# Five of nine modulation vectors as dot products on the vector engine, with their weights transposed and the attention heads' steps in another order

## The reference

```python
mod = silu(c) @ w_ada + b_ada                    # 6 vectors of 1024: sh1 sc1 g1 sh2 sc2 g2
h = rmsnorm(x, norm1_g) * (1 + sc1) + sh1
q, k, v, u = split(h @ w_in)                     # 4 heads with two maps each; u goes to the SSM
att = softmax(q0 k0) - lam * softmax(q1 k1)      # causal
attn_out = rmsnorm(att @ v, subln_g) * (1 - lambda_init)
z = gelu(ssm(u));  ssm_out = z * sigmoid(z @ w_glu + b_glu)
x = x + g1 * (concat(attn_out, ssm_out) @ w_out)
h = rmsnorm(x, norm2_g) * (1 + sc2) + sh2
x = x + g2 * moe(h)                              # 32 experts, each token goes to its top 4
x = rmsnorm(x, final_g)
shift, scale, gate = split(silu(c_2) @ w_mod_2 + b_mod_2)     # 3 more vectors
...                                              # second block: RG-LRU, dilated attention, merge
return rmsnorm(x + gate * (merged @ w_o), g_final_2)
```

## Time and profile before

| | us |
|---|---|
| median of 3 runs | 2116.95 (2116.36 to 2120.26) |
| profiled execution | 2112.3, span 2111.0 |
| PE busy | 2021.6 (96%) |
| DVE busy | 583.1 (28%) |
| ACT busy | 410.5 (19%) |

### The profile page before, as it was taken

The page is one execution under the profiler, slowest core; times in us unless marked ns, Lnnn a source line. Parts: engine busy times, 40 slices in busy tenths (PEclk is TensorE's granted clock), DMA queues, the critical chain, the costliest instruction groups (busy, mean ns, idle before and its releaser), DMA issues.

```text
span 2111.0 us, 36756 instructions
## 1 busy us (share of the span) xinstructions
PE 2021.6 (96%) x16085; PEld 908.0 (43%) x16085; DVE 583.1 (28%) x1166; ACT 410.5 (19%) x849; POOL 53.0 (3%) x54
## 2 busy tenths in 40 slices
PE   7999998999999999999999999989999999999998
PEld 3454444333443333434334334355444444444443
DVE  4994434211111111101101111142454444300002
ACT  2212432110111010101101101012333353300001
POOL 0000000000000000000000000030000000000000
PEclk9999999999999999999999999989999999999999
DMA  8455795999899999999999999971222211122201
GB/s 321 140 193 192 268 340 222 401 420 363 326 415 413 411 404 415 409 410 402 408 413 406 408 410 416 407 269 72 92 72 66 73 62 64 55 76 80 76 34 70
DMA packets 107153, 553.80 MB, mean 262 GB/s; under 512 B 12848, under 2 KB 24112, under 8 KB 57200
## 3 DMA queue, kind: packets, MB, share of 16 engines
q1 hardware_dynamic: 86880, 517.36, 61.9%
q10 hardware_dynamic: 14560, 17.28, 2.4%
q0 software_dynamic: 5552, 16.78, 2.3%
HBM read 526.73 MB, written 26.35 MB: 262 GB/s over the span
## 4 chain that ended last, share of the span: by engine, by line
PE 67%; SPq 16%; DMA 13%; DVE 2%; ACT 2%; issue 1%; POOL 0%; ACTq 0%; DVEq 0%; POOLq 0%
SPq L374 15%; PE psum L834 15%; PE psum L1007 13%; PE psum L1014 10%; PE psum L503 7%; PE psum L842 6%; DMA arena<-in_w 6%; DMA ring<-in_w 3%; PE psum L1077 3%; PE psum L967 2%; PE psum L476 1%; DMA ring<-in_mod_slabs 1%; DMA ring<-in_v_slabs 1%; PE psum L828 1%; PE psum L1055 1%
## 5 line engine op out<-in xcount | busy, mean ns | idle before, releaser
L834 PE MATMUL psum<-arena,ring 128*32 128x512 f32 x4096 | 452.9, 593 | 19.5 <-DMA arena<-in_w 19.0
L1007 PE MATMUL psum<-h_t,ring 128*128 128x512 f32 x640 | 278.6, 592 | 0.2 <-ACT arena L1383 0.2
L834 PEld LDWEIGHTS psum<-arena,ring 128*32 128x32 f32 x4096 | 134.4, 110 | 333.7 <-issue 331.3
L842 PE MATMUL psum<-arena,h_t 128*32 128x256 f32 x3840 | 217.4, 383 | 8.6 <-DMA arena<-in_w 7.4
L1310 ACT ACTIVATE ring<-psum,mods,gain 128x64 f32<-128x64 f32 (+2 forms) x264 | 85.8, 430 | 647.4 <-PE psum L820 647.4
L1879 DVE TENSOR_SCALAR h_t<-psum 128x512 f32<-128x512 f32 (+2 forms) x33 | 27.9, 845 | 613.8 <-PE psum L834 613.8
L1007 PEld LDWEIGHTS psum<-h_t,ring 128*128 128x128 f32 x640 | 120.4, 190 | 146.4 <-issue 145.9
L842 PEld LDWEIGHTS psum<-arena,h_t 128*32 128x32 f32 x3840 | 123.2, 111 | 93.8 <-DMA arena<-in_w 12.8
L834 PE MATMUL psum<-ring 128*32 128x512 f32 x1344 | 149.2, 593 | 6.4 <-DMA ring<-in_w 6.4
L503 PE MATMUL psum<-h_t,ring 128*128 128x512 f32 x256 | 116.1, 608 | 5.6 <-ACT h_t L1128 5.6
L1014 PE MATMUL psum<-h_t,ring 128*128 128x512 f32 x256 | 112.6, 593 | 1.4 <-ACT work L1192 1.4
(11 more groups left out here) (426 smaller groups left out, 1681.4 us busy)
## 6 DMA issues: line engine op xcount, KB each, us to landing
arena<-in_w SPq DMA_DIRECT2D x288, 1024.0 KB, 28.4
ring<-in_w SPq DMA_DIRECT2D x96, 1024.0 KB, 29.9
ring<-in_mod_slabs SPq DMA_DIRECT2D x16, 2048.0 KB, 9.1
ring<-in_turn_slabs SPq DMA_DIRECT2D x40, 512.0 KB, 3.4
ring<-in_merge_slabs SPq DMA_DIRECT2D x32, 512.0 KB, 3.3
ring<-in_proj_slabs SPq DMA_DIRECT2D x24, 512.0 KB, 3.7
y_rows<-arena SPq DMA_DIRECT2D x1, 10752.0 KB, 35.4
y_rows<-work ACTq DMA_DIRECT2D x70, 64.0 KB, 7.8
```

Of the source, the lines that this page charges most:

```text
L834: mm = pe.matmul(psum[32 * j:32 * j + 32, g, :], x_e[:, c * tokens + g * TG:c * tokens + g * TG + TG], slot[s][:, j * S:(j + 1) * S], star ...
L842: mm = pe.matmul(psum[32 * j:32 * j + 32, 6 + g // 2, (g % 2) * 256:(g % 2) * 256 + 256], h_e[:, g * 256 + half * P + 32 * c:g * 256 + hal ...
L1007: mm = pe.matmul(psum[:, bank, :], ring[:, s, k, :], h_t[:, k, :], start=(k == 0), stop=(k == KT - 1))
```

## The change

Modulations 0 to 3 stay as they were (`ROWS_TO = 4`). For 4 to 8 the weights come transposed (`dot_slabs`, 40 of 128x1024: one output feature on each partition, the 1024 inputs along it). PE spreads each of the two conditions over all partitions (`c_row`), ACT keeps it in `ring` slots 10 and 11, and DVE makes each column of `mods` with one multiply and add over 1024 elements (`dots`), 18 among the heads and 22 in the mix loop. The 40 loads go through slots 4 to 7 one at a time.

```diff
-TURN = 3
-TURNS = 7
+TURN = 7
+TURNS = 3
+        c_rows = [ring[:, 10 + n, :, :].rearrange("p k n -> p (k n)") for n in range(2)]
-        early = [arena[:, 4096 * n:4096 * n + 4096] ...
+        early = [arena[:, 8192 * n:8192 * n + 4096] ...
-        MIX_AT = [4, 5, 2, 3, 0, 1, 2, 3]
+        MIX_AT = [4, 6, 2, 3, 0, 1, 2, 3]
# SP
-            for i in range(12):
-                load_slab_of(8 + i)
-                load_mod_half((i + 5) // 2, (i + 5) % 2)
-            load_mod_half(8, 1)
-            (zeroing of y_rows in one transfer)
+            for n, at in zip(range(8, 11), ((2, 1), (3, 0), (3, 1))):
+                load_slab_of(n)
+                load_mod_half(*at)
+            def load_dots(*numbers):
+                for n in numbers:
+                    if n < 4:
+                        sp.wait_ge(sem("mod halves used"), len(MOD_HALVES))
+                    else:
+                        sp.wait_ge(sem("dots"), n - 3)
+                    sp.dma_start(ring[:, 4 + n % 4, :, :], io["dot_slabs"][n]...).then_inc(sem(f"slot {4 + n % 4} loaded"), 16)
+            load_slab_of(11)
+            load_dots(0, 1, 2, 3)
+            for n in range(12, 16):
+                load_slab_of(n)
             sp.wait_ge(sem("arena zeroed"), 1)
+            clear_blocks(0, 6)
+            load_slab_of(16)
+            load_dots(4, 5, 6, 7)
+            load_slab_of(17)
+            clear_blocks(6, 12)
+            load_dots(8, 9, 10, 11)
+            load_slab_of(18)
+            clear_blocks(12, MAXO)
+            load_dots(12, 13, 14, 15)
+            load_slab_of(19)
...
-            sp.wait_ge(sem("mod turned"), 18)
-            load_first(0, 1, 2, 3, 4, 5)
+            sp.wait_ge(sem("s5 y"), 4)
+            load_first(0, 2)
+            load_dots(16, 17, 18, 19)
+            load_first(3, 8)
+            load_dots(20, 21, 22, 23)
+            load_first(9)
+            load_dots(24, 25, 26, 27)
+            sp.wait_ge(sem("glu"), 4)
+            load_first(1)
             sp.wait_ge(sem("head mixed"), 4)
-            for n in range(20, 23):
+            for n in range(20, 24):
                 load_slab_of(n)
-            load_slab_of(23)
-            load_first(7, 8, 9, 6, 10, 11)
+                if n < 23:
+                    load_dots(*range(4 * n - 52, 4 * n - 48))
+            load_first(6, 10, 11)
+            sp.wait_ge(sem("dots"), 8 * (9 - ROWS_TO))
+            load_first(4, 5, 7)
# PE: first norm
-            pe.wait_ge(sem("tables loaded"), 16)
-            for _ in range(6): (product of 256 columns, not read)
-            rms_sum(0, h_t)
+            pe.wait_ge(sem("ready for idle products"), 1)
+            for _ in range(8): (product of 256 columns of zeros, not read)
+            pe.wait_ge(sem("tables loaded"), 16)
+            for k in range(KT):
+                pe.wait_ge(sem("norm squares"), k + 1)
+                mm = square_sum(k, k == 0, k == KT - 1)
             mod_row(0, 0)
+            pe.wait_ge(sem("row scales"), 1)
+            spread_scales(first_scale, 4)
             mod_row(1, 0)
...
             u_half(0, 0)
-            u_half(1, 0)
             mod_row(0, 1)
             mod_row(1, 1)
+            u_half(1, 0)
# PE: the list of the second part from slab 7 on, after
+            slab(7); scores_of(0); mod_row(3, 1); slab(8); mod_columns(3); c_row(0)
+            s5_output(0); slab(9); s5_output(1); slab(10); c_row(1); s5_output(2); slab(11)
+            turn_p(0); scores_of(1); slab(12); s5_output(3); turn_v(0); head_out(0)
+            slab(13); head_sum(0); turn_p(1); scores_of(2); slab(14); turn_v(1); head_out(1)
+            gate_of_s5(0); head_sum(1); gate_of_s5(1); turn_p(2); scores_of(3); slab(15)
+            turn_v(2); head_out(2); gate_of_s5(2); head_sum(2); gate_of_s5(3)
+            (router shift); turn_p(3); mixed_without_last(16); turn_v(3); head_out(3)
+            mixed_without_last(17); head_sum(3); mixed_without_last(18)
# ACT: its list there, after
+            keep_c(0); keep_slab(9); gelu_tanh(0); exps_of_head(0); keep_slab(10); keep_c(1); gelu_tanh(1)
+            keep_slab(11); keep_turned(1); gelu_tanh(2); (load w_glu); keep_slab(12); gelu_tanh(3)
+            exps_of_head(1); keep_v(0); head_squares(0); keep_slab(13); head_root(0); keep_turned(2)
+            keep_slab(14); exps_of_head(2); keep_v(1); head_squares(1); keep_gate(0); head_root(1)
+            keep_gate(1); keep_turned(3); keep_slab(15); exps_of_head(3); keep_v(2); head_squares(2)
+            keep_gate(2); head_root(2); keep_gate(3); (router shift); keep_turned(4); keep_v(3)
# DVE
-            dve.wait_ge(sem("mod halves used"), 4)
+            dve.wait_ge(sem("mod halves used"), MOD_HALVES.index((1, 0)) + 1)
+            def dots(first, past):
+                for n in range(first, past):
+                    g, k = ROWS_TO + n // 8, n % 8
+                    which = 0 if g < 6 else 1
+                    dve.wait_ge(sem("pair kept"), kept[("c", which, 1)])
+                    (wait for the load of dot n)
+                    weights = ring[:, 4 + n % 4, :, :].rearrange("p k n -> p (k n)")
+                    dve.tensor_tensor_reduce(weights, weights, c_rows[which], 1.0, 0.0, ALU.mult, ALU.add, mods[:, 8 * g + k:8 * g + k + 1]).then_inc(sem("dots"), 1)
+                    (after k == 7: add the bias)
+            states_of(0); states_of(1); gelu_begun(0); masked_head(0); states_of(2); gelu_begun(1)
+            gelu_ended(0); normal(0); states_of(3); gelu_begun(2); gelu_ended(1); gelu_begun(3)
+            masked_head(1); gelu_ended(2); dots(0, 3); normal(1); gelu_ended(3); head_mixed(0)
+            masked_head(2); dots(3, 7); normal(2); head_mixed(1); dots(7, 10); masked_head(3)
+            dots(10, 13); normal(3); (glu gates); head_mixed(2); dots(13, 18); head_mixed(3)
             for k in range(KT):
                 (residual step k of the mix loop, sums of squares)
+                dots(*((18, 22), (22, 26), (26, 30), (30, 34), (34, 37), (37, 40), (40, 40), (40, 40))[k])
# PE: overflow loop and behind the experts
             with pe.Fori(0, TURNS) as turn_at:
-                keep_on(1, 3)
...
+            keep_on(6, 0)
             turn_sum(0)
+            keep_on(3, 0)
             norm_sums(0)
# POOL: the 16 gathers
             for n in range(TT * TOPK):
+                if n == 3 * TOPK:
+                    pool.wait_ge(sem("slot 8 loaded"), 32)
```

More of the change, by code:

```diff
@@ L27 @@
 FF = 1024
+ROWS_TO = 4
 FIXED = 2
@@ L489, in mod_columns, with c_row, square_sum, spread_scales @@
                 mm.then_inc(sem("mod turned"), 2 if g > 1 else 1)
[L491 to L495, removed]
+            def c_row(n):
+                for half in range(2):
+                    bank = pair_bank(("c", n, half))
+                    for k in range(4):
+                        at = 8 * n + 4 * half + k
+                        mm = pe.matmul(bank[:, k * P:(k + 1) * P], c_act[:, at:at + 1].to_broadcast([P, P]), identity, start=True, stop=True, is_transpose=True, skip_group_check=True)
+                    mm.then_inc(sem("mod turned"), 1)
+            def square_sum(k, first, last):
+                for t in range(TT):
+                    mm = pe.matmul(psum[:, 1, t:t + 1], h_t[:, k, t * P:(t + 1) * P], ones[:, 0:1], start=(first and t == 0), stop=last, skip_group_check=True)
+                return mm
+            def spread_scales(scales, bank):
+                for t in range(TT):
+                    mm = pe.matmul(psum[:, bank, t * P:(t + 1) * P], scales[:, t:t + 1].to_broadcast([P, P]), identity, start=True, stop=True, is_transpose=True, skip_group_check=True)
+                mm.then_inc(sem("scale spread"), 1)
             def slab_part(n, src, bank, ks):
@@ L704, in tensor_engine @@
                 mm.then_inc(sem("glu"), 1)
-            mod_row(8, 1)
+            gate_of_s5(0)
+            head_sum(1)
+            gate_of_s5(1)
             turn_p(2)
-            mod_columns(8)
+            scores_of(3)
+            slab(15)
+            turn_v(2)
+            head_out(2)
+            gate_of_s5(2)
+            head_sum(2)
+            gate_of_s5(3)
             pe.wait_ge(sem("masks loaded"), 48)
@@ L737, in logit_part @@
                 return pe.matmul(psum[rows, 4, :], router[:, k, :], x_t[:, k, :], start=(k < 4), stop=(k >= 4), skip_group_check=True)
-            def square_sum(k, first, last):
-                for t in range(TT):
-                    mm = pe.matmul(psum[:, 1, t:t + 1], h_t[:, k, t * P:(t + 1) * P], ones[:, 0:1], start=(first and t == 0), stop=last, skip_group_check=True)
-                return mm
             for n in range(16, 24):
@@ L1084, in tensor_engine @@
             pe.wait_ge(sem("tile scale"), TT + 2)
[L1085 to L1087 removed]
+            spread_scales(last_scale, 0)
         def scalar_engine():
[L1091 to L1096 removed]
             pair = [0]
@@ L1140, in scalar_engine @@
             act.wait_ge(sem("norm sum"), 1)
-            root(rstd)
```

(11 more changed lines are left out.)

196 lines of the change are left out of this document (86 added, 110 removed).

## The result

The kernel after took 2124.6 us (median of 8 runs, 2121.7 to 2129.7) beside 2116.65 us of the kernel before on the same chip: ratio 1.0047, 95% interval 1.0035 to 1.0059. It is slower by 8 us. 2128 was forecast. Timed again on another chip it gave 1.0025 (1.0014 to 1.0036). The profiled execution took 2121.67 us, span 2120.3, against 2112.3 and 2111.0.

What follows compares the result with a forecast made beforehand. The first block was taken as bound by PE's instruction order, the expert stage by PE and weights. Early part -7.5, heads +8, mix +12.4, behind experts -2: +10.9 on 2116.95 gives 2128 us; own range 2119 to 2137, stated range 2104 to 2140.

Steps and rivals of the forecast that it cites:

- The mix loop, +12.4: Mix loop: slab 20 queued behind dot loads leaves PE idle 9.7 us plus 3.1 us slow clock; +12.4 us, bounds 0 and +16.
- The heads, +8: Heads: work removed -26.3, tidier waiting -9.8, new idle waits +29.9, slow clock +13.5; about +8 us, bounds -6 and +14.
- the clock, 13.5 us: Heads: PE slow after waits, 3.1 us for each of three long, 1.4 for each of three short; bounds 0 and 18.6.
- The early part, -7.5: To 75 us: earlier first scaling and DVE map products no longer waiting for both rows; -7.5 us, bounds -2.7 and -8.7.
- the first scaling 4 us earlier: First norm: the big reciprocal goes and the wait before it shrinks, so h is scaled 4 us earlier; bounds +3 to -8.
- rival (e): Early part: an idle stretch before the first norm keeps PE slow, gain only 2.7 us; 2133 us, inside the forecast.
- The second step: Early part: DVE's map products, starting at 46.85 before, start at 38 to 40 us; gain bounded at 8.9 us.
- Behind the experts, -2: After the expert stage: fewer loop turns, idle products moved, last four gathers held for V's second half; -2 us, bounds +2 and -6.
- (b): Heads and mix loop: the waits come but PE's clock stays up; total -5.7 us, 2111 us, chance 0.12.
- (a): PE-bound all the way: the heads' waits are covered after all; total -27 us, 2090 us, chance 0.10.
- (c): Mix loop: slab 20 comes in time, mix 0; total -1.5 us, 2115 us, chance 0.13.
- (d): Mix loop: dots cost double, DVE needs 65 us and PE waits; +15 us more, 2143 us, chance 0.11.

Runs made afterwards that it cites:

- experiments 2 and 3: On the kernel after: 2 loads slab 20 ahead of dots 24 to 27, ratio 1.0019; 3 also puts keep_v(i) ahead of the next head's exponentials, ratio 0.9941.
- experiment 8: The kernel after without the nine unread products behind the experts (six ahead of turn_sum(0), three behind it): 2128.0 us, ratio 1.0031 to the kernel before.

## Why the prediction was right, and where it was not

The sign and the forecast's time were right: 2128 forecast, 2124.6 measured, own range 2119 to 2137. In part that is luck: two wrong terms cancelled. By its steps:

**The mix loop, +12.4.** Measured +13.6. Slab 20 waited 11.38 us (9.7 forecast), and the 48 instructions behind it took 22.83 instead of 21.2, a clock cost of 1.6 where I put 3.1 (9.7 + 3.1 is 12.8, not the 12.4 of the forecast). Later slabs ran without a wait, and a dot took 1.22 us. The place, the queue and the size were right. Read further, to the end, the step was incomplete: putting slab 20 ahead of dots 24 to 27 doesn't win the 12 us back, since dots 20 to 23 still hold it and routing's stores are next in that traffic (experiments 2 and 3).

**The heads, +8.** Measured -0.1. Work removed and waits were right: 9.68, 6.51, 6.51 and 0.69 us ahead of `head_out` and 5.2 ahead of scores against 10.8, 6.5, 6.5, 1.2 with other small ones, and 4.9. The failed term is the clock, 13.5 us. Three `head_out` products took 4.25, 3.81 and 4.64 instead of 2.4, and one gate 0.9 more: 6.3 us. The waits of 1.5 to 2.1 us ahead of scores cost nothing at all: the slab behind each took 7.13. I had charged them 1.4 each from a row in which the wait was no longer. -26.3 - 9.8 + 29.9 + 6.3 is +0.1.

**The early part, -7.5.** Measured -2.1, outside my bounds. The step that failed is "the first scaling 4 us earlier"; it came 1.0 us earlier. The reciprocal went as forecast, but PE was later with the modulations that the scaling also needs. I had seen that small products might run at the lower clock and priced it only in rival (e), with a gain of 2.7 us, near the 2.1 measured. They did: 12.30 us for the sums and 3.44 instead of 1.92 for the row behind. What they ate was a gain that I had not counted: the unread products had moved from behind the load of `consts` into the wait for it, so that the sum could start at 9.8 instead of 14.92. With wide products `chunk_sums(0)` came 3.5 to 5.2 us earlier than before; with narrow ones between 2.1 earlier and 1.4 later. The second step, DVE's products at 38 to 40, was right (38.71), and worth nothing: from 32.45 on PE is never idle for more than 0.7 us at once until `chunk_sums(0)`, and its order, not DVE, says when row (1,1)'s modulations are ready. DVE waited 5.16 us for them.

**Behind the experts, -2.** Measured -2.9, with `turn_sum(0)` at 1.95 instead of 3.78. But the warm `turn_sum(0)` is not what gave it: without the unread products (experiment 8) it took 3.78 again and `norm_sums(0)` stood where it did. Counted from the end of the last expert product, the first `v_rows` started at 32.0 us (31.4 before); the gain is at the second, which had waited 2.22 us and taken 10.20 and now takes 7.11 without a wait. That the held gathers did this wasn't tested.

**Table load.** The price from the Trainium skill (ScalarE: Activation LUTs, "What ACT_TABLE_LOAD costs"), 2.66 us, would have put 1.4 more on each of two waits. The load begins at 220.82 and the first exponential at 222.11, 1.29 us later; the waits were 6.51 as the rows said.

**The sum, and the rivals.** Two errors cancelled: the heads were 8 us better than forecast, the early part 5.4 worse, and the other stages 1 us. The time was met better than its terms; what carried the sign are the waits of the heads and of slab 20, which came as charted. (b), the clock stays up, was right for half of the clock term. (a) and (c) fell with the waits, (d) with the dot's 1.22 us.

## What to carry to other kernels

When work is taken off the busiest engine, chart what it had covered: here 28 us of products went, and waits of 23.4 us for a copy on ACT's queue and 11.4 us for a slab on SP's gave more than that back, while moving three copies made the kernel 0.65% faster than before. When a load is moved forward in a queue, follow the bytes that it displaces to the next small transfer on the path: the slab's own wait fell by 4.5 us, and no gain in the time could be told. A narrower form of a product is not a cheaper one if PE's clock stays low while it runs.

## What the runs showed of the hardware

- 32 one-column products with their weight loads, PE shown busy 100%: the granted clock read 0.92 from 9 to 12 us and 0.50 (1.2 GHz) from there to 24; 256-column products in between (seven of 1.2 us) didn't raise it. With 512-column products in the same place it stayed at 1.00 in two profiles, and in two it was at 0.50 for some 3 us and back at 1.00 by 15 us.
- Waits of 1.56 to 2.09 us ahead of scores left the clock at 1.00; those of 6.5 and 9.7 us brought it to 0.50. The length doesn't decide alone: in the kernel before, products behind waits of 1.48 and 2.22 us ran at the lower clock.
- The start of `second_bias` behind the empty overflow loop came 5 to 6 us after the last expert product, or 12 to 13, by what stands ahead in PE's program (one profile for each of four kernels, with and without 28 unread products); in time that was 0.25% in two pairs, at the edge of the noise.
- The stores of 0.5 MB landed in 3.7 us (median) where SP's queue ran dry beside them, in 6.9 to 8.3 in the kernels before and after, and in 10.5 where ten 1 MB loads were in it.
